# Products of the first token group by both parts of the moving operand at once, in a two-layer fp32r transformer kernel

## What is computed

```python
def swiglu(x, w_gate, w_up, w_down):
    return (silu(x @ w_gate) * (x @ w_up)) @ w_down     # 1024 -> 2816 -> 1024
...
xp = layer_norm(DEEPNORM_ALPHA * xp + 0.5 * swiglu(xp, *f1), ln_g[layer, 0], ln_b[layer, 0])
xp = layer_norm(DEEPNORM_ALPHA * xp + mix_p, ln_g[layer, 1], ln_b[layer, 1])
xp = layer_norm(DEEPNORM_ALPHA * xp + 0.5 * swiglu(xp, *f2), ln_g[layer, 2], ln_b[layer, 2])
```

## Time and profile before

| | |
|---|---|
| median of 3 runs | 2528.83 us (2525.87 to 2530.12) |
| the profiled execution | 2529.85 us, its span 2528.2 us |
| PE busy | 2406.3 us (95%) |
| DVE busy | 1628.0 us (64%) |
| ACT, POOL busy | 1086.1, 458.9 us |
| mean granted clock | 0.982 |

### The profile page before, as it was taken

The page is one execution under the profiler, slowest core; times in us unless marked ns, Lnnn a source line. Parts: engine busy times, 40 slices in busy tenths (PEclk is TensorE's granted clock), DMA queues, the critical chain, the costliest instruction groups (busy, mean ns, idle before and its releaser), DMA issues.

```text
span 2528.2 us, 46326 instructions
## 1 busy us (share of the span) xinstructions
PE 2406.3 (95%) x18811; PEld 2268.4 (90%) x18811; DVE 1628.0 (64%) x2536; ACT 1086.1 (43%) x1663; POOL 458.9 (18%) x532
## 2 busy tenths in 40 slices
PE   7999999999998999999999999999999889999998
PEld 6988998999787777789999999999999889999997
DVE  4787776665764555567686566466656585587555
ACT  3433455433553333443254534554433537354333
POOL 4896800002100111200111101021001000121000
PEclk9999999999999999999899999999999999999999
DMA  8667776445346777644566556555555556555553
GB/s 179 176 177 190 205 198 192 125 117 143 116 136 207 221 239 226 164 123 128 142 175 175 164 148 208 169 153 150 154 149 148 169 165 215 156 158 146 150 150 96
DMA packets 676278, 417.31 MB, mean 165 GB/s; under 512 B 31555, under 2 KB 639683, under 8 KB 676067
## 3 DMA queue, kind: packets, MB, share of 16 engines
q1 hardware_dynamic: 669538, 393.98, 54.1%
q0 software_dynamic: 6528, 20.37, 2.5%
HBM read 395.51 MB, written 18.78 MB: 164 GB/s over the span
## 4 chain that ended last, share of the span: by engine, by line
PE 78%; DVE 12%; issue 3%; ACT 3%; DMA 2%; SPq 2%; POOL 0%; POOLq 0%; ACTq 0%; DVEq 0%
PE ps L256 21%; PE ps L257 20%; PE ps L258 20%; DVE w_lo L251 4%; PE ps L881 2%; PE ps L882 2%; PE ps L883 2%; ACT w_hi L242 2%; PE ps L2280 1%; PE ps L1593 1%; PE ps L1642 1%; DMA w_raw<-in_ffn_w_up 1%; DVE x L531 1%; PE ps L1614 1%; DVE h_lo L435 1%
## 5 line engine op out<-in xcount | busy, mean ns | idle before, releaser
L251 DVE TENSOR_TENSOR w_lo<-w_raw,w_hi 128x1024 fp32r<-128x1024 f32 (+1 forms) x648 | 825.0, 1278 | 623.9 <-ACT w_hi L242 620.9
L256 PE MATMUL ps<-x_hi,w_hi 128*128 128x256 f32 (+1 forms) x3200 | 969.3, 303 | 49.4 <-DVE w_lo L251 35.9
L257 PE MATMUL ps<-x_lo,w_hi 128*128 128x256 f32 (+1 forms) x3200 | 955.9, 299 | 0.0
L258 PE MATMUL ps<-x_hi,w_lo 128*128 128x256 f32 (+1 forms) x3200 | 955.5, 299 | 0.0
L242 ACT ACTIVATE w_hi<-w_raw 128x1024 fp32r<-128x1024 f32 (+1 forms) x648 | 669.6, 1035 | 553.8 <-PE ps L258 399.5
L256 PEld LDWEIGHTS ps<-x_hi,w_hi 128*128 128x128 f32 x3200 | 616.2, 193 | 68.4 <-DVE w_lo L251 53.6
L257 PEld LDWEIGHTS ps<-x_lo,w_hi 128*128 128x128 f32 x3200 | 616.7, 193 | 1.1 <-issue 0.2
L258 PEld LDWEIGHTS ps<-x_hi,w_lo 128*128 128x128 f32 x3200 | 616.1, 193 | 0.0
L256 PE MATMUL ps<-h_hi,w_hi 128*128 128x256 f32 (+1 forms) x1408 | 423.9, 301 | 12.3 <-DVE w_lo L251 9.5
L257 PE MATMUL ps<-h_lo,w_hi 128*128 128x256 f32 (+1 forms) x1408 | 414.5, 294 | 0.0
L258 PE MATMUL ps<-h_hi,w_lo 128*128 128x256 f32 (+1 forms) x1408 | 414.4, 294 | 0.0
(11 more groups left out here) (263 smaller groups left out, 2192.8 us busy)
## 6 DMA issues: line engine op xcount, KB each, us to landing
w_raw<-in_ffn_w_gate SPq DMA_DIRECT2D x176, 512.0 KB, 4.2
w_raw<-in_ffn_w_up SPq DMA_DIRECT2D x176, 512.0 KB, 3.9
w_raw<-in_ffn_w_down SPq DMA_DIRECT2D x128, 512.0 KB, 4.0
w_raw<-in_w_in_ab SPq DMA_DIRECT2D x56, 512.0 KB, 4.0
w_raw<-in_ffn_w_down SPq DMA_DIRECT2D x64, 384.0 KB, 3.5
arena<-in_cache_k SPq DMA_DIRECT2D x64, 256.0 KB, 4.2
arena<-in_cache_v POOLq DMA_DIRECT2D x64, 256.0 KB, 4.8
w_raw<-in_w_out_ab SPq DMA_DIRECT2D x16, 512.0 KB, 3.9
```

What stands on the lines that cost most here:

```text
L251: dve.tensor_tensor(T.w_lo[:, u % RING, 0:n], T.w_raw[:, u % RAW, 0:n], T.w_hi[:, u % RING, 0:n].bitcast(F32), ALU.subtract).then_inc(T.w_ ...
L256: pe.matmul(out, w_hi, m_hi, start=first, stop=False)
L257: pe.matmul(out, w_hi, m_lo, start=False, stop=False)
L258: return pe.matmul(out, w_lo, m_hi, start=False, stop=last)
```

## The change

The hi and lo parts of the moving operand become two halves of one tensor (`x_both`, `h_both`). A new function `columns_times_both` multiplies the hi weights by both halves with one matmul of 512 columns, which fills a whole PSUM bank, and the lo weights by the hi half with one of 256. Three matmuls and three weight loads become two. It is used in group A for the output pieces of all four SwiGLUs and of OA, and, with `F.both`, for gates and ups of f2a and f3a. Group B and the gates of f0a and f1a stay.

Someone has to add the two halves of the bank. For an output piece DVE adds the second half with a further operation. With `F.both`, DVE sums the halves of a gate (a reduce over pairs, PSUM to `gate`), ACT takes the tanh of that sum and writes it to PSUM, and DVE sums the halves of the up before the product. The remainder `h_lo` moves from DVE to GpSimd.

```diff
+def columns_times_both(T, pe, u, out, both, n, ready=None):
+
+    kt = T.pieces[u].shape[1]
+    for k in range(kt):
+        if ready is not None:
+            sem, value = ready
+            pe.wait_ge(sem.h, value + k + 1)
+        w_hi, w_lo = (w[:, u % RING, k * P:(k + 1) * P] for w in (T.w_hi, T.w_lo))
+        m = both(k)
+        if k:
+            pe.matmul(out[:, 0:n], w_lo, m[:, 0], start=False, stop=False)
+        mm = pe.matmul(out[:, 0:2 * n].rearrange("p (s n) -> p s n", s=2), w_hi, m, start=(k == 0), stop=(k == kt - 1))
+        if not k:
+            mm = pe.matmul(out[:, 0:n], w_lo, m[:, 0], start=False, stop=False)
     return mm
...
     for i, d, u, o in Q.steps():
         round_piece(T, act, u + LEAD)
         if d is None:
-            act.wait_ge(T.w_used.h, u + 1)
-            act.activation(T.gate[:, i % 2, 0:g.n], T.ps[:, T.banks[o], 0:g.n], ACT.Tanh, scale=0.5)\
-               .then_inc(T.tanh_done.h, 1)
+            if F.both:
+                act.wait_ge(T.gate_summed.h, Q.summed + i + 1)
+                act.activation(T.ps[:, T.banks[o], 0:g.n], T.gate[:, i % 2, 0:g.n], ACT.Tanh, scale=0.5)\
+                   .then_inc(T.tanh_done.h, 1)
+            else:
+                act.wait_ge(T.w_used.h, u + 1)
+                act.activation(T.gate[:, i % 2, 0:g.n], T.ps[:, T.banks[o], 0:g.n], ACT.Tanh, scale=0.5)\
+                   .then_inc(T.tanh_done.h, 1)
             round_piece(T, act, u + 1 + LEAD)
...
         rest_piece(T, dve, u + LEAD)
         if d is None:
+            gate, prod, hi = T.gate[:, i % 2, 0:g.n], T.prod[:, i % 2, 0:g.n], T.h_hi[:, i, 0:g.n]
+            ps_gate, ps_up = (T.ps[:, T.banks[o + s], :] for s in range(2))
+            if F.both:
+                dve.wait_ge(T.w_used.h, u + 1)
+                dve.tensor_reduce(gate, ps_gate.rearrange("p (s n) -> p n s", s=2), AX_X, ALU.add).then_inc(T.gate_summed.h, 1)
+                dve.wait_ge(T.gate_summed.h, Q.summed + i + 1)
             rest_piece(T, dve, u + 1 + LEAD)
-            gate, prod = T.gate[:, i % 2, 0:g.n], T.prod[:, i % 2, 0:g.n]
             dve.wait_ge(T.tanh_done.h, Q.tanh + i + 1)
-            dve.scalar_tensor_tensor(gate, gate, 1.0, T.ps[:, T.banks[o], 0:g.n], ALU.add, ALU.mult)\
-               .then_inc(T.silu_done.h, 1)
+            dve.scalar_tensor_tensor(gate, gate if not F.both else ps_gate[:, 0:g.n], 1.0, ps_gate[:, 0:g.n] if not F.both else gate,
+                                     ALU.add, ALU.mult).then_inc(T.silu_done.h, 1)
             dve.wait_ge(T.silu_done.h, Q.silu + i + 1)
             dve.wait_ge(T.w_used.h, u + 2)
-            dve.scalar_tensor_tensor(prod, gate, 0.5, T.ps[:, T.banks[o + 1], 0:g.n], ALU.mult, ALU.mult)\
+            if F.both:
+                if Q.h + i > 1:
+                    dve.wait_ge(T.h_done.h, Q.h + i - 1)
+                T.dve_chain(dve, dve.tensor_reduce(prod, ps_up.rearrange("p (s n) -> p n s", s=2), AX_X, ALU.add))
+            dve.scalar_tensor_tensor(prod, gate, 0.5, prod if F.both else ps_up[:, 0:g.n], ALU.mult, ALU.mult)\
                .then_inc(T.glu_done.h, 1)
             dve.wait_ge(T.glu_done.h, Q.glu + i + 1)
-            hi = T.h_hi[:, i, 0:g.n]
             dve.tensor_copy(hi, prod).then_inc(T.h_rounded.h, 1)
             dve.wait_ge(T.h_rounded.h, Q.rounded + i + 1)
-            dve.tensor_tensor(T.h_lo[:, i, 0:g.n], prod, hi.bitcast(F32), ALU.subtract).then_inc(T.h_done.h, 1)
+            if not F.both:
+                dve.tensor_tensor(T.h_lo[:, i, 0:g.n], prod, hi.bitcast(F32), ALU.subtract).then_inc(T.h_done.h, 1)
         else:
             xd = T.x[:, d, g.cols]
             dve.wait_ge(T.w_used.h, u + 1)
...
                 dve.wait_ge(T.affine_done.h, F.x_whole)
             else:
                 dve.wait_ge(T.res_done.h, Q.res_before + d + 1)
-            dve.scalar_tensor_tensor(xd, xd, 2.0 * ALPHA if Q.part == 0 else 1.0, T.ps[:, T.banks[o], 0:g.n],
-                                     ALU.mult, ALU.add).then_inc(T.res_done.h, 1)
+            last = dve.scalar_tensor_tensor(xd, xd, 2.0 * ALPHA if Q.part == 0 else 1.0, T.ps[:, T.banks[o], 0:g.n],
+                                            ALU.mult, ALU.add)
+            if g is A:
+                T.dve_chain(dve, last)
+                last = dve.tensor_tensor(xd, xd, T.ps[:, T.banks[o], g.n:2 * g.n], ALU.add)
+            last.then_inc(T.res_done.h, 1)
...
+        if d is None and Q.F.both:
+            n = Q.g.n
+            pool.wait_ge(T.h_rounded.h, Q.rounded + i + 1)
+            if i == 0 and Q.u:
+                pool.wait_ge(T.w_used.h, Q.u)
+            pool.tensor_tensor(T.h_lo[:, i, 0:n], T.prod[:, i % 2, 0:n], T.h_hi[:, i, 0:n].bitcast(F32), ALU.subtract)\
+                .then_inc(T.h_done.h, 1)
...
-        F2A, F1B = Ffn(A, ffn_2, N2A.ready, N2A.affine + KT), None
+        F2A, F1B = Ffn(A, ffn_2, N2A.ready, N2A.affine + KT, True), None
...
-        F3A = Ffn(A, ffn_3, N4A.ready, N4A.affine + KT)
+        F3A = Ffn(A, ffn_3, N4A.ready, N4A.affine + KT, True)
```

More of the change, by code:

```diff
@@ L181, in open_trunk @@
     T.y_moved = [count("y_moved0"), count("y_moved1")]
+    T.gate_summed = count("gate_summed")
     T.tanh_done, T.silu_done, T.glu_done, T.h_rounded, T.h_done = map(
@@ L201, in sb @@
         return ctx.enter_context(T.nc.sbuf_tensor(f"{name}_{len(T.pieces)}", shape, dt))
-    T.h_hi, T.h_lo = sb("h_hi", [P, 8, NMAX], F32R), sb("h_lo", [P, 8, NMAX], F32R)
+    T.h_both = sb("h_both", [P, 2, 8, NMAX], F32R)
+    T.h_hi, T.h_lo = T.h_both[:, 0], T.h_both[:, 1]
     T.gate, T.prod = sb("gate", [P, 2, NMAX]), sb("prod", [P, 2, NMAX])
@@ L341, with __init__ @@
 class Ffn:
-    def __init__(self, g, w, x_ready, x_whole):
-        self.g, self.w, self.x_ready, self.x_whole = g, w, x_ready, x_whole
+    def __init__(self, g, w, x_ready, x_whole, both=False):
+        self.g, self.w, self.x_ready, self.x_whole, self.both = g, w, x_ready, x_whole, both
 class FfnPart:
@@ L357, in __init__ @@
             c.take(n) for c in (T.tanh_done, T.silu_done, T.glu_done, T.h_rounded, T.h_done))
+        self.summed = T.gate_summed.take(n) if F.both else None
         self.res_before = None if part == 0 else F.res
@@ L390, in ffn_tensor @@
                 bank = bank_of(T, pe, o + s)
[L391 to L394, removed]
+                ready = (T.x_ready, F.x_ready) if i == 0 and s == 0 and Q.part == 0 else None
+                if F.both:
+                    columns_times_both(T, pe, u + s, T.ps[:, bank, :], lambda k: T.x_both[:, :, k, g.cols], g.n, ready)\
+                        .then_inc(T.w_used.h, 1)
+                else:
+                    columns_times(T, pe, u + s, T.ps[:, bank, 0:g.n], lambda k: T.x_hi[:, k, g.cols],
+                                  lambda k: T.x_lo[:, k, g.cols], True, True, ready).then_inc(T.w_used.h, 1)
         else:
@@ L397, in ffn_tensor @@
             bank = bank_of(T, pe, o)
-            columns_times(T, pe, u, T.ps[:, bank, 0:g.n], lambda k: T.h_hi[:, k, 0:g.n],
-                          lambda k: T.h_lo[:, k, 0:g.n], True, True,
-                          (T.h_done, Q.h) if d == 0 else None).then_inc(T.w_used.h, 1)
+            ready = (T.h_done, Q.h) if d == 0 else None
+            if g is A:
+                columns_times_both(T, pe, u, T.ps[:, bank, :], lambda k: T.h_both[:, :, k, 0:g.n], g.n, ready)\
+                    .then_inc(T.w_used.h, 1)
+            else:
+                columns_times(T, pe, u, T.ps[:, bank, 0:g.n], lambda k: T.h_hi[:, k, 0:g.n],
+                              lambda k: T.h_lo[:, k, 0:g.n], True, True, ready).then_inc(T.w_used.h, 1)
         yield
 def ffn_scalar(T, act, Q):
-    g = Q.g
+    F, g = Q.F, Q.g
     for i, d, u, o in Q.steps():
@@ L593, in __init__ @@
         self.u, self.o = len(T.pieces), len(T.banks)
+        self.both = g is A and not self.gated
         self.res = T.res_done.take(KT)
@@ L623, in out_tensor @@
             bank = bank_of(T, pe, o + s)
-            columns_times(T, pe, u + s, T.ps[:, bank, 0:g.n], lambda k: T.x_hi[:, k, g.cols],
-                          lambda k: T.x_lo[:, k, g.cols], True, True).then_inc(T.w_used.h, 1)
+            if R.both:
+                columns_times_both(T, pe, u + s, T.ps[:, bank, :], lambda k: T.x_both[:, :, k, g.cols], g.n)\
+                    .then_inc(T.w_used.h, 1)
+            else:
+                columns_times(T, pe, u + s, T.ps[:, bank, 0:g.n], lambda k: T.x_hi[:, k, g.cols],
+                              lambda k: T.x_lo[:, k, g.cols], True, True).then_inc(T.w_used.h, 1)
         yield
@@ L657, in out_vector @@
         dve.wait_ge(T.affine_done.h, R.x_whole)
-        dve.scalar_tensor_tensor(T.x[:, d, g.cols], T.x[:, d, g.cols], 2.0 * ALPHA if R.gated else ALPHA, y, ALU.mult,
-                                 ALU.add)\
-           .then_inc(T.res_done.h, 1)
+        xd = T.x[:, d, g.cols]
+        last = dve.scalar_tensor_tensor(xd, xd, 2.0 * ALPHA if R.gated else ALPHA, y, ALU.mult, ALU.add)
+        if R.both:
```

(3 more changed lines are left out.)

7 lines of the change are left out of this document (5 added, 2 removed).

## The result

The changed kernel takes 2603.48 us (2600.62 to 2604.67), against 2527.62 us before in the same comparison: ratio 1.0297 (1.0282 to 1.0313), 76 us slower. The forecast was 2566 us, slower by 37. Direction and mechanism were right; the size was half of what came. The time lies inside the stated range of 2543 to 2605 us, but by 1.5 us only, and that is luck: the terms of the sum missed by 39 us together.

A forecast was written before the change was run, and what follows sets the result against it. PE was taken to bound the kernel (busy 95%, 78% of the chain). Gates 30, part ends 8, output additions 4, PE's saving -5 gave +37 us: 2566 us, range 2543 to 2605.

The forecast's parts named there:

- The ring: f2a and f3a units: DVE reduce, ACT tanh, ACT rounding, DVE subtraction wait in turn; 6.36 us a unit against 5.76.
- The half-pace rival: Gate and up reduces of f2a and f3a read pairs 256 apart at half pace, 1.36 us each; 2626 us, chance 6%.
- The sum over the six stretches: Gates and ups of f2a.0, f2a.1, f2a.2, f3a.0, f3a.1 and f3a.2 together take 30 us longer.
- DVE's side work: f2a and f3a gates: DVE's busy time less 3.94 us a unit, added on top of 6.36 us a unit.
- Handovers: Ends of the six parts: first output piece waits for GpSimd's last h_lo, some 1.4 us each, +8 us.
- The 1.2 us: At each part's end, PE's first blocks hide about 1.2 us of h_lo's lateness, estimated from 7 blocks of 0.35 us.
- Output pieces with PE's saving: SwiGLU output pieces and OA: DVE's second additions cost +4 us, PE's fewer matmuls give back 5 us.
- GpSimd goes second: f2a and f3a units: DVE's even subtraction precedes GpSimd's h_lo; rival, GpSimd first, 0.67 us more in 44 units, 2587 us, 13%.
- Faster or unchanged: Two whole-kernel rivals: PE's saving reaches the end, 2514 us, chance 7%; or almost no change, 2531 us, chance 6%.
- The unchanged case: New waits cost only in f2a.2 and f3a.2, where PE alone sets the pace; 2531 us, chance 6%.
- Reduces of 415 ns: Lower bound for each gate or up reduce in f2a and f3a, against 0.68 us taken; 24 us less, 2544 us.

The follow-up runs named there:

- Cutting the ring: Changed kernel with one line moved: in f2a and f3a ACT rounds the odd piece before the tanh; 2553.24 us, ratio 1.0098.
- the markers: Kernel before, ACT's tanh in f2a and f3a waiting for DVE work added between its subtractions: one element set, 2551.65 us; two copies, 2578.22 us.

## Why the prediction was right or wrong

**The ring: right.** Unit 6.44 us against 6.36 forecast, DVE's wait 1.51 against 1.46, reduces 0.68 and 0.69 against 0.68, at pairs 256 apart. The half-pace rival is out. Cutting the ring returned 50 us.

**The sum over the six stretches: 30 us forecast, 52 measured.** The term that was mis-sized is DVE's side work, which I took as its busy time less 3.94 us a unit. With 6.44 us a unit taken off, the measured stretches leave 18.8 us in f2a.0 (12.5 by my working), 4.9 in f2a.1 (4.2), 17.9 in f3a.0 (10.5), 41.1 in f3a.1 (29.6) and 4.8 in f3a.2 (3.9). Busy time leaves out the waits and gaps that go with side work, and my allowances for them were too small: f2a.0 +3 against +8.6, f3a.0 +1 against +5.2, f3a.1 +9 against +19.5. The other three were close: +7, +4 and +6 forecast, +8.1, +4.0 and +7.0 measured.

In f3a.1 DVE was often the bound already, and there before and after can be compared directly. In the kernel before a unit's two subtractions stand back to back without a wait, and its own operations end where the side work begins:

```profile
2055.34 2.36 DVE L251 TENSOR_TENSOR w_lo<-w_raw,w_hi 128x1024 fp32r<-128x1024 f32 x2
...
2059.20 0.35 DVE L2389 TENSOR_TENSOR arena<-arena 128x192 f32<-128x192 f32 x1
```

That is 3.86 us; in the changed kernel it is 6.43:

```profile
2092.14 1.22 DVE L253 TENSOR_TENSOR w_lo<-w_raw,w_hi 128x1024 fp32r<-128x1024 f32 x1
...
2098.57 0.43 DVE L2450 TENSOR_TENSOR arena<-arena 128x256 f32<-128x256 f32 x1
```

The difference is 2.57 us. From even subtraction to even subtraction, five of the eight steps of f3a.1 grew by 3.07 to 3.15 us: these 2.57, and 0.55 for the side step that meets GpSimd's remainder. The granted clock of the stretch was 0.85 after 0.93 before, but these two terms leave nothing for it in the five. The other three grew by 0.88, 2.10 and 0.89 us. Three subtractions of the kernel before had waited for ACT there, and waits of that kind stayed in the changed kernel beside the ring instead of making room for it; the longest of each:

```profile
2102.57 2.44 DVE L251 TENSOR_TENSOR w_lo<-w_raw,w_hi 128x1024 fp32r<-128x1024 f32 x2 [3.52 <-ACT w_hi L242]
...
2164.60 1.23 DVE L253 TENSOR_TENSOR w_lo<-w_raw,w_hi 128x1024 fp32r<-128x1024 f32 x1 [3.23 <-ACT w_hi L244]
```

My working had such waits (9.5 us before) as free room.

**Handovers: size low, cause mostly wrong.** I said 8 us, by GpSimd's late remainder. PE waited 15 us, and nearly as long with DVE computing it; with the ring cut open 7.2 and 4.6. So the main cause is the ring's lag at the end of each part. The 1.2 us that PE's first blocks were to cover did not follow either: the seven blocks of 0.35 us named for it make 2.45.

**Output pieces with PE's saving: -1 forecast (4 - 5), +9 measured.** The saving was overrated: with no additions at all, PE's new form saves 5.6 us in the whole kernel, not 15.6. The forecast had a block of x at 0.346 us, by the 0.2263 us of a 512-column matmul of the projection; blocks took 0.348 to 0.355. Whether the two halves make the difference is not shown. By the marks the second additions cost about 1 to 2 us each in more places than the three that I named: f2a.0, the pieces just after it, and OA.

**GpSimd goes second: right.** The subtraction stayed at 1.22 us and the remainder took 1.77, so that rival is out. The Trainium skill (SBUF — State Buffer, SBUF: two separate sides) says that whoever starts first holds the shared ports for the whole instruction; by that rule, the trace agrees at 1361.69 (DVE) and 1361.74 (GpSimd).

**Faster or unchanged: wrong rivals.** The unchanged case wanted the ring to be hidden where side work runs, and f3a.1 lost most. Reduces of 415 ns were not tried. As an estimate they would make the turn 6.44 - 2 x 0.27 = 5.90 us, between the markers' 5.43 and 6.19, which cost 23 and 48 us.

## What to carry to other kernels

Before adding an operation between two engines, draw the waits as a ring and add its length, start to start; compare it with the pace of the engine that sets the time, and not the busy shares. A ring inside a fixed queue also takes away the freedom to catch up: side work then adds to the turn in full, so price each stretch by the turn with and without the ring where that engine is already full. If a wait must be added, put whatever doesn't need it ahead of it in the queue; here one line was worth 50 us. And busy time doesn't tell how much room an engine has: its waits can stay where they are when work is added.
